# Two fused transformer blocks on one core: a reordered first block, a twelfth weight slot, and a second block that starts on rows that are not yet normalised

## The chip, the cores and the metric

The program runs on 1 core of one Trainium2 chip. The metric is the device time of one execution in microseconds (us). All arithmetic is 32-bit float. TensorE is called PE here, VectorE DVE, ScalarE ACT, GpSimd POOL and SyncE SP.

## The reference, cut to what matters

The input is x, 256 rows of 1024 features; 16 learned meta rows are put ahead of it for the first mixer.

```python
# block 1
h = concat(meta, x)                                   # 16 + 256 rows
p = rmsnorm(h, norm1_g) @ w_in                        # 1024 -> 6144: q f i og lx ly ga gb
o_a = hgrn2(q, f, i, og)                              # 4 heads of 128, gated linear recurrence
o_b = rglru(conv4(lx), ly)                            # two 128x128 products per block, then a scan
m = sigmoid(ga) * (o_a @ w_up_a) + sigmoid(gb) * (o_b @ w_up_b)
h = h + m @ w_out
h = h + moe(rmsnorm(h, norm2_g))                      # 32 experts, 2 per row, 6 MB of weights each
x = rmsnorm(h, final_g)[16:]
# block 2
p = rmsnorm(x, norm1_g_2) @ w_in_2                    # 1024 -> 7680: 3 q, 3 k, 3 v, uv, ga, gb
m = sigmoid(ga) * (attn(q, k, v) @ w_proj_attn) + sigmoid(gb) * (gmlp(uv) @ w_proj_sgu)
x = x + m @ w_out_2
x = x + (silu(n @ w_gate) * (n @ w_up)) @ w_down      # n = rmsnorm(x, norm2_g_2), 2816 wide
return rmsnorm(x, final_g_2)
```

Every expert is evaluated for the up to 32 rows routed to it, so all 201 MB of expert weights are read.

## The kernel before, in words

The order on each engine is written by hand, and every dependence is a named semaphore. SP issues nearly all weight loads, in units of 2 MB (`load`, L310). Block 1 has 18 units in a ring of 6 slots; the experts have 96 units, 12 for each group of four experts, in 11 slots (`NSLOT`, `MOE_SLOTS`), five of which lie in the work area and come free as block 1 ends; block 2 has 36 units in the ring again. A load into a slot waits for the semaphore of the work that read it last (`used1`, `used2`, `unit_used`). SP waits for `params_issued` before its first load, that is, until ACT has issued the loads of x, of the meta rows and of all small parameters.

Block 1 starts with a normalisation of the rows: ACT squares and sums each tile of rows (L1000), POOL turns the sum into the reciprocal root (L442, L444), DVE scales the rows (L1258), PE transposes them (L504), DVE copies them out of PSUM with the gain (L1278) into `hnT`. Then PE goes through the units: `project_rows` (L537) makes rows, 16 meta rows and two tiles of 128, `project_cols` (L528) makes feature-major columns in four chunks, each in one of PSUM banks 0 to 3 and each evacuated by ACT (`evac`, L1015). A matmul of 32-bit floats is two PE instructions. Between the units stand the recurrence's own products: the end keys and values (L552, L557, with DVE copies L1351, L1354, L1360 between them), the levels (L577), the heads' outputs, their sums of squares (L605), and the 16 LRU products (L617), each followed by a sigmoid of ACT (L1081). The columns `gb` are projected after the LRU products. `up_a` (L628) goes to banks 0 to 3 and waits for the last evacuation; `up_b` (L636) goes to banks 4 to 7. DVE merges the two (`merge`, L1468 to L1470), and `out_projection` (L651) waits for all eight merged columns:

```python
            pe.wait_ge(S("evac"), n_out[0])
            pe.wait_ge(S("oa_ready"), 1)
...
                        if t == 0 and k == 0:
                            pe.wait_ge(S(ready), total)
```

Routing follows, and then the experts, four at a time: gate, up, gather for the next four, down, and a weighted sum into banks 4 to 7 (`combine`, L727). The last group's down weights come in column halves (L755).

After the last `combine` DVE copies the result to `h` (L1672), the final norm of block 1 is applied to the rows (L1677), then the first norm of block 2 is taken with squares, root, scaled rows, transposes and gain, into `hn2`, and ACT makes a copy `hn2c` with columns sorted by residue class (L1171). Only then does block 2's first unit start (L537). The evacuated q and k rows are rotated by DVE and transposed (L844); attention, the gated unit, merge, output projection and feed-forward (L961, L1801, L651) follow.

## Time and profile before

| | us |
|---|---|
| median of 3 runs | 1340.3 (1337.79 to 1340.61) |
| the profiled execution, own time | 1339.59 |
| its span | 1337.8 |
| PE busy | 1117.2 (84%) |
| DVE busy | 253.9 (19%) |
| ACT busy | 179.3 (13%) |
| POOL busy | 18.3 (1%) |
| chain that ended last: PE | 69% of the span |
| chain that ended last: DMA | 23% of the span |

Busy time is summed over the span; the chain follows the work back from the last instruction, so it says which engine or transfer set the end at each moment. The chain lies on PE up to 350.5 us, on the expert loads up to 769.1 us, and on PE again to the end, with short pieces of DVE, ACT and POOL between them.

### The profile page before, as it was taken

The numbers are of one execution on the slowest core, as the hardware profiler recorded it, in microseconds if no ns is written. First come the engines' busy times: TensorE is split into PE (matmuls) and PEld (weight loads), VectorE is DVE, ScalarE is ACT, GpSimd is POOL, SyncE is SP. The second block draws the span as 40 slices with busy tenths as digits, with TensorE's granted clock in tenths as the row PEclk, the third lists the DMA queues.
The fourth block names the chain that finished last, engine by engine and source line by source line (L and its number), as shares of the span: only waits on it lengthen the run. The fifth ranks groups of instructions, "written<-read, shape, count | busy, mean of one in ns | idle before, by whom it ended". The sixth has DMA issues, their size and how long they took to land.

```text
span 1337.8 us, 12093 instructions
## 1 busy us (share of the span) xinstructions
PE 1117.2 (84%) x5319; PEld 696.7 (52%) x5319; DVE 253.9 (19%) x585; ACT 179.3 (13%) x354; POOL 18.3 (1%) x47
## 2 busy tenths in 40 slices
PE   6989999898965666465575679999999889999997
PEld 2778988765422212121231234444688648888643
DVE  4233243423110000000000041101353310000000
ACT  2213325101100000000000031111333010000000
POOL 1000000000000000000000010000000000000000
PEclk9989999997977867787787889999999989999999
DMA  8732334484799999999999995336223334453200
GB/s 299 243 126 91 110 108 163 185 319 184 309 428 427 429 425 427 430 426 428 428 429 427 394 348 182 126 126 219 90 101 126 126 108 146 139 178 137 95 16 16
DMA packets 89631, 318.31 MB, mean 238 GB/s; under 512 B 8684, under 2 KB 34392, under 8 KB 78824
## 3 DMA queue, kind: packets, MB, share of 16 engines
q1 hardware_dynamic: 81536, 313.53, 59.9%
q10 hardware_dynamic: 8040, 3.96, 1.1%
q8 instruction: 44, 0.72, 0.2%
q14 instruction: 11, 0.09, 0.0%
HBM read 316.43 MB, written 1.05 MB: 237 GB/s over the span
## 4 chain that ended last, share of the span: by engine, by line
PE 69%; DMA 23%; DVE 3%; ACT 2%; SPq 1%; issue 1%; ACTq 0%; POOL 0%; POOLq 0%; DVEq 0%
PE bank L537 13%; PE bank L961 12%; PE bank L528 11%; PE bank L651 10%; PE bank L708 5%; DMA ring<-in_w_gate 5%; DMA ring<-in_w_up 5%; DMA ring<-in_w_down 4%; PE bank L859 4%; DMA arena<-in_w_gate 4%; DMA arena<-in_w_down 3%; DMA arena<-in_w_up 2%; PE bank L941 2%; PE bank L636 2%; PE bank L746 2%; SPq L310 1%
## 5 line engine op out<-in xcount | busy, mean ns | idle before, releaser
L708 PE MATMUL bank<-ring,arena 128*32 128x512 f32 x512 | 128.0, 733 | 61.3 <-DMA ring<-in_w_up 27.7
L537 PE MATMUL bank<-ring,arena 128*128 128x512 f32 (+1 forms) x400 | 175.4, 598 | 1.6 <-DVE arena L1278 1.6
L708 PE MATMUL bank<-arena 128*32 128x512 f32 x384 | 128.0, 738 | 55.7 <-DMA ring<-in_w_gate 21.2
L528 PE MATMUL bank<-arena,ring 128*128 128x256 f32 (+1 forms) x704 | 157.8, 386 | 1.2 <-DVE arena L1360 1.2
L961 PE MATMUL bank<-arena,ring 128*128 128x256 f32 x704 | 154.7, 383 | 0.8 <-DVE arena L1278 0.8
L528 PEld LDWEIGHTS bank<-arena,ring 128*128 128x128 f32 x704 | 134.6, 192 | 23.0 <-DVE arena L1360 1.5
L961 PEld LDWEIGHTS bank<-arena,ring 128*128 128x128 f32 x704 | 135.5, 193 | 20.0 <-DVE arena L1278 1.2
L651 PE MATMUL bank<-ring,arena 128*128 128x512 f32 x304 | 131.2, 593 | 6.5 <-DVE arena L1470 5.4
L537 PEld LDWEIGHTS bank<-ring,arena 128*128 128x128 f32 (+1 forms) x400 | 73.9, 187 | 97.1 <-issue 94.6
L651 PEld LDWEIGHTS bank<-ring,arena 128*128 128x128 f32 x304 | 57.5, 190 | 78.8 <-issue 78.8
L708 PEld LDWEIGHTS bank<-ring,arena 128*32 128x32 f32 x512 | 31.8, 132 | 113.3 <-issue 113.3
L708 PEld LDWEIGHTS bank<-arena 128*32 128x32 f32 x384 | 31.2, 132 | 96.0 <-issue 96.0
L746 PE MATMUL bank<-ring,arena 128*32 128x512 f32 x224 | 61.8, 700 | 19.2 <-DMA arena<-in_w_down 13.2
L746 PE MATMUL bank<-arena 128*32 128x512 f32 x224 | 61.8, 729 | 18.8 <-DMA ring<-in_w_down 12.7
L1015 ACT ACTIVATE arena<-bank 128x256 f32<-128x256 f32 (+3 forms) x85 | 37.8, 448 | 275.2 <-PE bank L537 149.9
L859 PE MATMUL bank<-arena,ring 128*128 128x256 f32 x256 | 59.4, 385 | 0.8 <-ACT arena L1015 0.8
L1589 DVE TENSOR_TENSOR h<-h,bank 128x512 f32<-128x512 f32 x8 | 5.5, 689 | 274.0 <-PE bank L708 260.6
L859 PEld LDWEIGHTS bank<-arena,ring 128*128 128x128 f32 x256 | 47.3, 190 | 10.3 <-issue 4.1
L1000 ACT ACTIVATE arena<-h 128x1024 f32<-128x1024 f32 x12 | 12.7, 1055 | 223.6 <-DVE h L1481 209.7
L1801 DVE TENSOR_TENSOR arena<-arena,bank 128x256 f32<-128x256 f32 x22 | 9.3, 422 | 146.4 <-ACT arena L1232 146.4
L746 PEld LDWEIGHTS bank<-ring,arena 128*32 128x32 f32 x224 | 15.0, 126 | 40.7 <-issue 40.0
L746 PEld LDWEIGHTS bank<-arena 128*32 128x32 f32 x224 | 15.3, 131 | 37.4 <-issue 37.4
(273 smaller groups left out, 871.2 us busy)
## 6 DMA issues: line engine op xcount, KB each, us to landing
ring<-in_w_in SPq DMA_DIRECT2D x27, 2048.0 KB, 9.2
ring<-in_w_up SPq DMA_DIRECT2D x20, 2048.0 KB, 35.0
ring<-in_w_gate SPq DMA_DIRECT2D x16, 2048.0 KB, 34.8
arena<-in_w_gate SPq DMA_DIRECT2D x16, 2048.0 KB, 33.9
ring<-in_w_down SPq DMA_DIRECT2D x14, 2048.0 KB, 32.6
arena<-in_w_down SPq DMA_DIRECT2D x14, 2048.0 KB, 35.5
arena<-in_w_up SPq DMA_DIRECT2D x12, 2048.0 KB, 32.8
ring<-in_w_ffn_gate SPq DMA_DIRECT2D x11, 1024.0 KB, 5.3
```

What stands on the lines that cost most here:

```text
L310: sp.dma_start(dst, src).then_inc(S(f"landed{s}"), 16)
L528: last = mm(b[:, 0:n], w3(s, KC)[:, k, m * P:(m + 1) * P], hn[:, k, lo:lo + n], start=(k == 0), stop=(k == KC - 1))
L537: last = mm(b[0:n, :], hn[:, k, lo:lo + n], w3(s, KC)[:, k, :], start=(k == 0), stop=(k == KC - 1))
L636: last = mm(bank[4 + m // 2][:, (m % 2) * T:(m % 2 + 1) * T], w3(up_b[k // 4], 4)[:, k % 4, m * P:(m + 1) * P], ly[:, k, :], start=(k == 0 ...
L651: last = mm(bank[2 * t + half][:, :], src[:, k, t * P:(t + 1) * P], w3(slots[k // 4], 4)[:, k % 4, half * 512:(half + 1) * 512], start=(k ...
L708: last = mm(bank[b][e * CAP:(e + 1) * CAP, :], xgT[:, k, e * CAP:(e + 1) * CAP], w[e][:, k, :], start=(k == 0), stop=(k == KC - 1))
L746: last = mm(bank[2 + half][e * CAP:(e + 1) * CAP, :], hT[:, k, e * CAP:(e + 1) * CAP], w[e][:, k, half * 512:(half + 1) * 512], start=(k = ...
L859: last = mm(b[:, 0:T], w3(gate_slot[0], KC)[:, k, (n % 4) * P:(n % 4 + 1) * P], hn2[:, k, :], start=(k == 0), stop=(k == KC - 1))
L941: last = mm(bank[lo + m // 2][:, (m % 2) * T:(m % 2 + 1) * T], w3(su, 4)[:, k, m * P:(m + 1) * P], src[:, k, :], start=(k == 0), stop=(k = ...
L961: last = mm(b[:, q * T:(q + 1) * T], w3(su, 2 * KC)[:, KC * q + k, (c % 2) * P:(c % 2 + 1) * P], hn2[:, k, :], start=(k == 0), stop=(k == ...
L1000: A_(junk[tile][0:n, :], src[0:n, tile, :] if tile < NT else meta[0:n, :], ACT.Square, accum_out=stat[0:n, col + tile:col + tile + 1]).the ...
L1015: A_(dst, src, func).then_inc(S("evac"), 1)
```

## The change

In block 1, x is loaded by SP ahead of the weights, and the first unit in two halves; the wait for the small parameters goes. PE transposes the raw rows, DVE puts the gain on them (`rT`), and the first unit is projected from these, with the row scale applied by ACT at the evacuation. The normalised `hnT` is made from `rT` by DVE with the scale spread over partitions by a product with ones. The meta rows' unit is projected in four column groups of PE, whose partial sums stay apart and are added by the key-value product with the keys repeated four times. The end-key transposes and products stand between chunks of the units `lx0` and `lx1`. Half of `gb0` is projected ahead of the LRU products. `up_a` goes to banks 4 to 7 and `up_b` to 0 to 3. ACT evacuates `gb1` before the LRU's square root. Both output projections start once six merged columns are there, and take the second tile's two halves one after the other.

A twelfth slot of 2 MB is its own tensor; room comes from a work area 80 words smaller and from `dynamic_dma_scratch_size=256` in place of the default.

At the end of the experts, the first 512 features of the result are copied, transposed raw and scaled by gain before the last expert unit is projected. Block 2's unit 0 starts on these; the other 512 features are transposed between its steps. The row scale (final norm times first norm of block 2) is applied by ACT at evacuation for units 0 to 6. DVE makes `hn2c` from `hn2` with the spread scale after unit 1, and PE waits for it (`classed`) before unit 2; `hn2` itself is scaled later, and PE waits for that before unit 9.

The diff, cut to its core (several semaphores are merged or renamed too, and the branch for more than 32 rows per expert is adapted; it isn't taken in the profiled execution):

```diff
-NSLOT = 11
-MOE_SLOTS = [0, 1, 6, 7, 8, 2, 3, 9, 4, 5, 10]
-B2_SLOTS = [4, 5, 0, 1, 2, 3]
-WORK = 4432
+NSLOT = 12
+MOE_SLOTS = [11, 0, 1, 6, 7, 8, 2, 3, 9, 4, 5, 10]
+B2_SLOTS = [0, 1, 2, 3, 4, 5]
...
+DMA_SCRATCH = 256
...
-            sp.wait_ge(S("params_issued"), 1)
+            for t in range(NT):
+                sp.dma_start(h[:, t, :], A["x"][0, t * P:(t + 1) * P, :]).then_inc(S(f"x_in{t + 1}"), 16)
...
                     sp.wait_ge(S(used1(u - RING)[0]), used1(u - RING)[1])
-                if name in W1_COL:
+                if u == 0:
+                    sp.dma_start(w3(s, KC)[:, 0:4, :], w1[:, 0:4, W1_COL[name]:W1_COL[name] + 512]) \
+                        .then_inc(S("half_landed"), 16)
...
-            turn_rows(((2, META), (0, P), (1, P)), "n1", xn, 3)
+            pe.wait_ge(S("gain_loaded"), 16)
+            tr(bank[7][:, 0:8], vecrows[0:8, :], ident[0:8, 0:8]).then_inc(S("vec_turned"), 1)
+            for t in range(NT):
+                pe.wait_ge(S(f"x_in{t + 1}"), 16)
+                for half in range(2):
+                    for c in range(4):
+                        k = 4 * half + c
+                        last = tr(bank[2 * t + half][:, c * P:(c + 1) * P], h[:, t, k * P:(k + 1) * P], ident[:, :])
+                    last.then_inc(S("x_turned"), 1)
+            pe.wait_ge(S("vec_loaded"), 16 * (len(VEC_ROWS) - 1))
+            tr(bank[6][:, 0:NVR], vecrows[0:NVR, :], ident[0:NVR, 0:NVR]).then_inc(S("vec_turned"), 1)
...
+            def project_meta(s):
+
+                b = out_bank()
+                for k in range(0, KC, 4):
+                    for c in range(4):
+                        last = mm(b[32 * c:32 * c + 32, :], hnT[:, k + c, 0:32], w3(s, KC)[:, k + c, :],
+                                  start=(k == 0), stop=(k == 4))
+                last.then_inc(S("projected"), 1)
+
+            pe.wait_ge(S("half_landed"), 16)
+            for t in range(NT):
+                b = out_bank()
+                pe.wait_ge(S("x_scaled"), 2 * (t + 1))
+                for k in range(KC):
+                    if t == 0 and k == 4:
+                        take1(0)
+                    last = mm(b[:, :], rT[:, k, t * P:(t + 1) * P], w3(0, KC)[:, k, :], start=(k == 0), stop=(k == KC - 1))
+                last.then_inc(S("projected"), 1)
+                if t == 0:
+                    turn_meta()
+                else:
+                    spread_rstd(0)
+                    spread_rstd(1)
+            pe.wait_ge(S("norm_done"), 2)
+            pe.wait_ge(S("hn_scaled"), NT)
+            project_meta(0)
             project_cols(take1(1), hnT, 0, TT)
             project_cols(take1(2), hnT, META, T)
-            project_cols(take1(3), hnT, 0, TT)
-
...
+            s3 = take1(3)
+            project_cols(s3, hnT, 0, TT, (0, 1))
+            turn_k(0)
+            project_cols(s3, hnT, 0, TT, (2, 3))
+            turn_k(1)
+            s4 = take1(4)
+            project_cols(s4, hnT, 0, TT, (0,))
+            kv(0)
+            kv(1)
+            project_cols(s4, hnT, 0, TT, (1, 2, 3))
...
-            project_cols(take1(4), hnT, 0, TT)
...
+            s11 = take1(11)
+            project_cols(s11, hnT, META, T, (0, 1))
             take1(10)
...
-            project_cols(take1(11), hnT, META, T)
+            project_cols(s11, hnT, META, T, (2, 3))
             project_cols(take1(12), hnT, META, T)
...
-            pe.wait_ge(S("evac"), n_out[0])
...
+            pe.wait_ge(S("lru_gates"), 16)
             pe.wait_ge(S("oa_ready"), 1)
...
-            last.then_inc(S("up_a"), 1)
-            pe.wait_ge(S("lru_gates"), 16)
+            last.then_inc(S("projected_a"), 1)
+            pe.wait_ge(S("evac"), n_out[0])
             pe.wait_ge(S("ob_ready"), 1)
             up_b = [take1(14), take1(15)]
             for m in range(KC):
+                if m >= 4:
+                    pe.wait_ge(S("merged"), m - 3)
                 for k in range(KC):
...
+                last.then_inc(S("projected_b"), 1)
...
-                for t in range(NT):
+                for k in range(total):
+                    if k % 4 == 0:
+                        slots.append(take(u0 + k // 4))
+                    pe.wait_ge(S(ready), max(k + 1, min(6, total)))
+                    for half in range(2):
+                        last = mm(bank[half][:, :], src[:, k, 0:P], w3(slots[k // 4], 4)[:, k % 4, half * 512:(half + 1) * 512],
+                                  start=(k == 0), stop=(k == total - 1))
+                last.then_inc(S("out_" + ready), 1)
+                for half in range(2):
                     for k in range(total):
-                        if t == 0 and k % 4 == 0:
-                            slots.append(take(u0 + k // 4))
-                        if t == 0 and k == 0:
-                            pe.wait_ge(S(ready), total)
-                        for half in range(2):
-                            last = mm(bank[2 * t + half][:, :], src[:, k, t * P:(t + 1) * P],
-                                      w3(slots[k // 4], 4)[:, k % 4, half * 512:(half + 1) * 512],
-                                      start=(k == 0), stop=(k == total - 1))
+                        last = mm(bank[2 + half][:, :], src[:, k, P:T],
+                                  w3(slots[k // 4], 4)[:, k % 4, half * 512:(half + 1) * 512],
+                                  start=(k == 0), stop=(k == total - 1))
                     last.then_inc(S("out_" + ready), 1)
...
-            combine((0,))
+            combine((0,)).then_inc(S("combined"), 1)
+
+            def turn_half(half, done="raw_turned"):
+
+                for t in range(NT):
+                    pe.wait_ge(S("y_added"), 1 if half == 0 else 2 + t)
+                    for c in range(4):
+                        last = tr(bank[half + t][:, c * P:(c + 1) * P], h[:, t, (4 * half + c) * P:(4 * half + c + 1) * P],
+                                  ident[:, :])
+                    last.then_inc(S(done), 1)
+
+            turn_half(0)
             down_columns(1, 2, take_moe(m + 11)).then_inc(S("unit_used"), 1)
             pe.wait_ge(S("y_copied"), 2 * QUADS - 1)
...
-            turn_rows(((0, P), (1, P)), "n3", [xn2[:, 0, :], xn2[:, 1, :]], 2)
-            pe.wait_ge(S("norm_done"), 2 * ROWS["n3"] + 4)
...
+            s0 = take2(0)
+            b0, b1 = out_bank(), out_bank()
+            pe.wait_ge(S("raw_done"), 2)
+            steps(s0, b0, 0, (0, 1))
+            turn_half(1)
+            steps(s0, b0, 0, (2, 3))
+            steps(s0, b1, 1, (0, 1, 2, 3))
+            pe.wait_ge(S("raw_done"), 3)
+            steps(s0, b0, 0, (4, 5, 6, 7)).then_inc(S("projected"), 1)
+            pe.wait_ge(S("raw_done"), 4)
+            steps(s0, b1, 1, (4, 5, 6, 7)).then_inc(S("projected"), 1)
...
             for n in range(11):
-                if n == 7:
+                if n == 2:
                     pe.wait_ge(S("classed"), 1)
-                project_rows(take2(n), tiles, hn2c if n in (7, 8) else hn2)
+                if n == 9:
+                    pe.wait_ge(S("classed"), 2)
+                if n:
+                    project_rows(take2(n), tiles, hn2c if n in (7, 8) else hn2)
+                if n == 1:
+                    pe.wait_ge(S("s_diag"), 2)
+                    for t in range(NT):
+                        last = mm(bank[7][:, t * P:(t + 1) * P], ones[:, :], s_diag[:, t, :], start=True, stop=True)
+                    last.then_inc(S("s_spread"), 1)
...
+            for t in range(NT):
+                dve.wait_ge(S("r_spread"), t + 1)
+                dve.wait_ge(S("x_scaled"), 2 * NT)
+                v.tensor_tensor(hnT[:, :, META + t * P:META + (t + 1) * P], rT[:, :, t * P:(t + 1) * P],
+                                bc(bank[(7, 3)[t]][:, 0:P], [P, KC, P], 1), ALU.mult).then_inc(S("hn_scaled"), 1)
...
-            act.wait_ge(S("lru_under"), 1)
-            A_(lrut, lrut, ACT.Sqrt).then_inc(S("lru_root"), 1)
             for c in range(4):
                 evac(gb[:, 4 + c, :], ACT.Sigmoid, n=T)
+            act.wait_ge(S("lru_under"), 1)
+            A_(lrut, lrut, ACT.Sqrt).then_inc(S("root"), 1)
...
+            def hold(half, t):
+
+                return v.tensor_copy(h[:, t, half * 512:(half + 1) * 512], bank[4 + 2 * t + half][:, :])
+
+            def scale_half(half, turned, done):
+                for t in range(NT):
+                    dve.wait_ge(S(turned[0]), turned[1] + t)
+                    v.tensor_tensor(hn2[:, 4 * half:4 * half + 4, t * P:(t + 1) * P],
+                                    bank[half + t][:, :].rearrange("p (c t) -> p c t", c=4),
+                                    bc(gains3[:, 4 * half:4 * half + 4], [P, 4, P], 2), ALU.mult).then_inc(S(done), 1)
+
             for q in range(QUADS):
...
+                if q + 1 == QUADS:
+                    dve.wait_ge(S("combined"), QUADS)
+                    hold(0, 0)
+                    hold(0, 1).then_inc(S("y_added"), 1)
+                    scale_half(0, ("raw_turned", 1), "raw_done")
...
+            dve.wait_ge(S("combined"), QUADS + 1)
+            for t in range(NT):
+                hold(1, t).then_inc(S("y_added"), 1)
+            scale_half(1, ("raw_turned", 3), "raw_done")
...
+                if n == 0:
+                    dve.wait_ge(S("s_spread"), 1)
+                    link(v.tensor_copy(sbc, bank[7][:, 0:T]))
+                    for k in range(KC):
+                        last = v.tensor_tensor(hn2c[:, k, :].rearrange("p (c j a) -> p c j a", c=4, j=4),
+                                               hn2[:, k, :].rearrange("p (a j c) -> p c j a", j=4, c=4),
+                                               sbc.rearrange("p (a j c) -> p c j a", j=4, c=4), ALU.mult)
+                    last.then_inc(S("classed"), 1)
+            dve.wait_ge(S("projected"), B1_OUTS + 14)
+            v.tensor_tensor(hn2, hn2, bc(sbc, [P, KC, T], 1), ALU.mult).then_inc(S("classed"), 1)
```

## Rows read from the trace of the kernel before

**Rows 1.** The page: busy tenths of the DMA engines in 40 slices of the span.

```profile
DMA  8732334484799999999999995336223334453200
```

**Rows 2.** Windows: us, busy PE, PEld, DVE, ACT, POOL; granted clock, DMA share, GB/s.

```profile
15.00:20.00 5.00, 4.21 (x13) 2.12 (x12) 3.67 (x12) 1.00 (x3) 0.16 (x1) 1.00 1.05 387
...
340.00:350.00 10.00, 9.15 (x87) 3.22 (x90) 1.45 (x3) 3.00 (x3) 0.00 (x0) 1.00 0.55 205
...
400.00:500.00 100.00, 59.81 (x420) 22.60 (x408) 6.25 (x12) 4.42 (x7) 0.00 (x0) 0.80 1.01 428
```

**Rows 3.** Timeline of the start: start us, us, queue or engine, line, instruction, idle before.

```profile
7.64 61.91 SPq L310 DMA_DIRECT2D ring<-in_w_in  x9
...
17.88 22.79 PE L537 MATMUL bank<-ring,arena 128*16 128x512 f32 x48 [0.79 <-DVE arena L1278]
```

**Rows 4.** DMA issues: tile, engine, count, KB each, median us to landing.

```profile
h<-in_x ACTq DMA_DIRECT2D x2, 512.0 KB, 4.0
```

**Rows 5.** The chain that ended last, around the keys: start us, us, what.

```profile
40.67 43.15 PE bank L528 x192
...
83.82 0.45 PE bank L552 x4
...
92.81 16.83 PE bank L528 x64
...
113.21 13.82 PE bank L528 x64
```

**Rows 6.** Timeline of the end of the first mixer, the stretch 196 to 287 us.

```profile
196.41 1.88 PE L605 MATMUL bank<-arena,ones 128*128 128x512 f32 x4
...
202.02 6.83 ACT L1081 ACTIVATE arena<-bank,vec 128x272 f32<-128x272 f32 x16
...
207.40 1.22 DVE L1442 TENSOR_TENSOR arena<-arena 128x1024 f32<-128x1024 f32 x1
...
208.17 27.79 PE L528 MATMUL bank<-arena,ring 128*128 128x256 f32 x128
...
222.59 1.28 ACT L1089 ACT_TABLE_LOAD   x1
...
230.64 2.43 DVE L1449 TENSOR_TENSOR arena<-arena 128x2176 f32<-128x2176 f32 x1 [20.31 <-ACT arena L1091]
...
235.63 2.02 ACT L1094 ACTIVATE arena<-arena 128x2176 f32<-128x2176 f32 x1 [3.72 <-DVE arena L1451]
...
240.22 15.66 PE L628 MATMUL bank<-arena,ring 128*128 128x256 f32 x64 [4.26 <-ACT arena L1015]
...
245.49 2.29 DVE L1461 TENSOR_TENSOR arena<-arena 128x2048 f32<-128x2048 f32 x1
...
286.22 13.97 PE L651 MATMUL bank<-ring,arena 128*128 128x512 f32 x32 [2.71 <-DVE arena L1470]
```

**Rows 7.** Timeline of SP's queue: the first load that reuses an expert slot.

```profile
343.62 0.33 SPq L310 DMA_DIRECT2D ring<-in_w_down  x1
```

**Rows 8.** The chain that ended last, from the last expert load to block 2.

```profile
769.08 1.97 PE bank L755 x16
...
773.84 1.30 DVE h L1672 x2
...
786.62 27.73 PE bank L537 x64
```

**Rows 9.** Timeline of PE: the combine of the first column half.

```profile
765.52 1.98 PE L727 MATMUL bank<-h,arena 128*128 128x512 f32 x4
```

**Rows 10.** Timeline of SP's queue: the last expert loads and the first of block 2.

```profile
752.02 5.16 SPq L310 DMA_DIRECT2D arena<-in_w_down  x2
758.24 129.55 SPq L310 DMA_DIRECT2D ring<-in_w_in  x13
```

**Rows 11.** Timeline of block 2's end: a merge step, the last projection.

```profile
1061.65 0.42 DVE L1468 TENSOR_TENSOR arena<-arena,bank 128x256 f32<-128x256 f32 x1 [0.99 <-PE bank L941]
...
1254.23 75.77 PE L651 MATMUL bank<-ring,arena 128*128 128x512 f32 x176 [1.02 <-DVE arena L1801]
```

More of the change, by code:

```diff
@@ L366, in _ @@
                 elif s == 9:
[L367 removed]
+                    sp.wait_ge(S("projected_b"), KC)
                 elif s == 10:
@@ L1050, in _ @@
             level_exp(1)
-            for c in range(4):
-                evac(lx[:, 4 + c, 3:3 + TT], ACT.Copy, n=TT)
+            for c in range(5, KC):
+                evac(lx[:, c, 3:3 + TT], ACT.Copy, n=TT)
             level_exp(2)
@@ L1074, in _ @@
             act.wait_ge(S("o_mean"), 1)
-            A_(rsn, rsn, ACT.Sqrt).then_inc(S("o_root"), 1)
+            A_(rsn, rsn, ACT.Sqrt).then_inc(S("root"), 1)
+            for c in range(2):
+                evac(gb[:, c, :], ACT.Sigmoid, n=T)
             for b in range(KC):
@@ L1365, in seg @@
+            dve.wait_ge(S("end_decay"), 3)
+            dve.wait_ge(S("state"), 1)
+            for hd in range(HEADS):
+                last = v.scalar_tensor_tensor(out=St[:, 1, hd, :], in0=St[:, 0, hd, :],
+                                              scalar=egA[:, hd:hd + 1], in1=bank[7][:, hd * P:(hd + 1) * P],
+                                              op0=ALU.mult, op1=ALU.add)
+            last.then_inc(S("state"), 1)
             def seg(ap, m):
```

284 lines of the change are left out of this document (165 added, 119 removed).

## The prediction, on record before the changed kernel ran

> **What bounds the kernel now.** I read the page first: the DMA engines are nearly full from slice 12 to slice 24 and less than half busy in most others [rows 1]. The windows say how full: between 400 and 500 us they move 428 GB/s and PE is busy for 59.8 of 100 us [rows 2]. So the span has three stages: block 1, bound by PE and by waits between engines; the expert loads, bound by transfers; block 2, bound by PE. Then I read the chain of waits in order of time, to see in each stage which wait ends last. A saving in block 1 counts only if it also lets the expert stream start earlier. It does: the stream's first reuse of a slot is issued at 343.62 us [rows 7], right after the first expert product, and the window 340 to 350 is at 205 GB/s, not full [rows 2]. From there to the last landing at 769.08 [rows 8] the stream never pauses. Block 1 sets when it starts, its bytes set how long it lasts, and the path from the last landing to block 2's first product comes in full.
>
> All sums are against the profiled execution, 1339.6 us with a span of 1337.8; the median of the three runs is 1340.3.
>
> **Price of a unit.** 64 PE instructions of 512 columns take 27.73 us [rows 8], so one tile of 128 rows (16 instructions) is 6.93 and a unit of two tiles 13.87. A unit of 256 columns is 13.82 [rows 5]. The chain's 43.15 us for f, q and lx0 [rows 5] less 13.82 leaves 14.66 for each unit of 272 columns.
>
> **The start.** Before, the weights are issued at 7.64 and the first product starts at 17.88; 48 instructions end at 40.67 [rows 3, 5]. Two tiles are 13.87 of these 22.79 us. The other 8.9 are the meta rows, which cost as many instructions as a full tile (6.93), and 2.0 at the lower pace of the first few. After: x is issued on SP at about 1 us and lands 4 us later [rows 4]. The half unit behind it (1 MB at the 387 GB/s of these weights [rows 2]) needs 2.7 us more. I add 1.5 for the small parameters that now move at the same time, and take 9.5 for the first product. The bounds: 8 with no such cost, and 11.5 if the present lag of 10.2 us from issue to product stays. The raw transposes and the gain on DVE lie beside that transfer. Then 13.9 + 2.0 for two tiles. DVE multiplies 2 x 1024 columns by the spread scale (1.22 each [rows 6]) with PE waiting, 2.6 with its semaphores. The meta unit is 16 instructions in four column groups, a shape that the last expert unit runs in 1.97 [rows 8]. End: 9.5 + 13.9 + 2.0 + 2.6 + 1.9 = 29.9, against 40.67. Gain 10.8 (8.8 to 12.5). ACT's squares and POOL's roots are done long before these two tiles end; their cover gone, each tile's root would cost about 1 us.
>
> **The end keys.** From 83.82 to the end of the next unit at 109.64 the chain takes 25.8 us, where the unit alone is 14.66: 9.0 of transposes and products with DVE copies between them, and 2.2 because the unit after them, on 16.83, begins at the low clock [rows 5]. After, DVE's copies lie beside half units of 7 us. What stays is PE's own work: two times four transposes and two times eight product instructions, by 0.45 for four [rows 5] some 2.7. Gain 8.4 (6 if the clock falls all the same). DVE now reaches the first level differences 7 us later in the unit, but the first level stands 9 us behind that and needs only four DVE steps and two exponentials.
>
> **The LRU stage.** Before: sums of squares end at 198.3, sixteen products run at ACT's pace (6.83 us for its 16 sigmoids) until gb starts at 208.17, its two units end at 235.96, PE idles 4.26 and `up_a` takes 15.66 instead of 13.8, to end at 255.9 [rows 6]. After: half of gb0 (6.9) from 198.1 hides the DVE mean and the square root; the products end about 211.4, the rest of gb at 232.2, and `up_a`, which no longer waits for the evacuation, at 246.0. Late next is `ob_ready`. ACT's exponentials start behind gb0's last evacuation at 218.8, take 8.05 as now (222.59 to 230.64), DVE 5.0, so `lru_under` is at 231.9; but ACT first evacuates the last gb chunk (232.6), loads the table (1.28) and takes the root (2.02): 235.9. From the root's end at 237.65 to `ob_ready` at 247.78 are 10.1 us now [rows 6]; after: 246.0. This meets `up_a`'s end with nothing to spare. Gain 9.9 (7.5 to 10.1).
>
> A switch of table costs 1.28 us by the trace [rows 6]. The Trainium skill (ScalarE: Activation LUTs, What ACT_TABLE_LOAD costs) puts 2.66 us on every switch, a drain included. By that `ob_ready` would come 1.4 us later and the gain would be 8.5; the sum goes by the trace.
>
> **First merge and output.** PE waits 2.71 us for the last two merges before `out_projection` [rows 6]; it now needs six of eight, which are there. At the end only one of two additions from PSUM is left; two copies of that shape take 1.30 [rows 8], and I take the same. Gain 2.7 + 0.6 = 3.3.
>
> Block 1 in all: 10.8 + 8.4 + 9.9 + 3.3 = 32.4.
>
> **The twelfth slot.** Slot 11 needs no wait, so it fills in block 1, where the DMA engines have room. At the first reuse twelve units have landed and not eleven: one unit of 2.097 MB at 428 GB/s [rows 2], 4.9 us. It is worth nothing if the stream turns out not to be full.
>
> **The seam.** L is the last landing (769.08). Now block 2's unit 1 starts at 786.62 + 13.87 = 800.5, which is L + 31.4. After: the first combine ends at 767.5 (L - 1.6) [rows 9], two copies 1.3 [rows 8], eight transposes 0.9: PE is free at L + 0.7, so the last unit starts 0.7 late and ends at L + 2.5. DVE copy 0.7, combine 2.0: L + 5.3. PE's own read of the overflow flag was hidden; 1 us for it (0 to 1.5): SP's queue reads the same flag between its last expert load (752.02 + 5.16) and block 2's first at 758.24, 1.06 us [rows 10]. The unit's 16 + 16 instructions 13.9, eight transposes 0.9, semaphores 0.2: L + 21.3. The unit's weights stand directly behind the last expert unit in SP's queue, 5.4 us at 387 GB/s: L + 5.4, in time. Norms, roots and `row_scale` run beside the unit. Gain 10.1; bounds 5, if PE starts it at the low clock and the flag costs more, and 10.6.
>
> **The new wait.** PE reaches unit 2 some 1.2 us after unit 1 (spread, eight transposes). DVE copies the spread scale and makes eight class-sorted products; 0.42 each is the nearest row [rows 11], 3.8 with the copy, from 0.5 us after unit 1. Price 3.1 us; 2.3 if they overlap, 6 if the sorted read is slower and the clock falls. Behind the wait are all later units of PE, and nobody else.
>
> **Block 2's end.** The same wait of 2.7 us before its `out_projection` goes, as do half the additions twice (0.6 each), and 1.0 before the last projection [rows 11]. Gain 4.9.
>
> **Sum.** 32.4 + 4.9 + 10.1 - 3.1 + 4.9 = 49.2. 1339.6 - 49.2 = 1290.4; I say 1291.
>
> **Rivals.**
> A. Block 1 gives back nearly a quarter of its gain, because the waits removed turn into others on DVE or ACT (start bound by the weights as now, `ob_ready` late, the clock low after the key products). By the low bounds: 8.8 + 6 + 7.5 + 3 = 25.3, so 1298. The tie at `ob_ready` speaks for it; against it, every engine but PE is under a third busy.
> B. The seam doesn't pay: PE runs unit 0 at the low clock in pieces and the `classed` wait costs 6: 5 + 3 us lost, 1299. With A, 1306.
> C. The raw start does nothing, since block 2's weights arrive too late. They come behind 2 MB of transfers at 387 GB/s; if unit 0 landed at L + 17, the present start, the gain of 10.1 would be gone: 1301. Speaks against it: the queue is in order and now block 2 waits for DVE and not for a load.
> D. Slower than before: the expert stream itself loses rate, because the slots, their addresses and the descriptor room change. 84 units follow the first reuse. It decides from 49.2 / 84 = 0.59 us per unit, 382 GB/s and below. At 350 GB/s a unit is 6.0 us: 1291 + 92 = 1383. The stream ran at 428 GB/s in eleven slots of two tensors alike, which speaks against.
> E. More than the sum: the start at 8, the tight waits all met: 1281 to 1284.
>
> **How the numbers follow.** Forecast (1285 to 1296) 0.55, A 0.14, B 0.10, C 0.06, A and B together 0.04, E 0.08, D 0.03. The bounds of the terms together are some 8 us on either side. The range runs from 1282 to 1304 and leaves out half of E, A with B, and D. Within 0.2% (2.7 us) is about what a measurement of this kernel can't tell from no change; to end there, A, B and C together wouldn't do. Faster 0.97, same 0.01, slower 0.02.
>
> **What would show it.** The first L537-type product near 9.5 us and unit f starting near 30; no gap of over 1 us at the keys; `up_b` starting near 226.6 (255.7 - 10.8 - 8.4 - 9.9); the first reuse of an expert slot near 311; full windows until about 732 (769.1 - 32.4 - 4.9); block 2's first product 6 to 7 us behind the last landing and unit 1 at 21; one new PE wait of 3 us on DVE before unit 2. Wrong would be: windows below 428 GB/s in the stream, DVE or ACT behind a new PE wait of over 2 us in block 1, or a granted clock of 0.5 in unit 0 of block 2.

## The result, and the profile after

The changed kernel takes 1307.8 us (median of 4 runs, 1306.26 to 1308.26), the kernel before 1340.2 in the same session: a ratio of 0.976, 95% interval 0.9743 to 0.9777. That is faster, as forecast, but 16.8 us above the 1291 and 3.8 above the range. The profiled execution took 1307.79 with a span of 1305.8; against 1339.59 it saves 31.8 where the sum said 49.2. So 17.4 us are to be found.

The expert stream is as it was, by the windows of the changed kernel (us, busy PE, PEld, DVE, ACT, POOL, granted clock, DMA share, GB/s), against 428 in [rows 2]:

```profile
400.00:500.00 100.00, 61.06 (x416) 24.02 (x420) 5.22 (x10) 4.88 (x7) 0.00 (x0) 0.81 1.01 427
```

The chain that ended last, first 100 us (start us, us, what):

```profile
5.67 5.15 DMA arena<-in_final_g
...
11.18 8.58 PE bank L600 x16
...
35.65 5.52 ACTq L1149
...
41.20 4.35 ACTq L1149
...
45.58 2.00 ACTq L1149
...
47.61 1.28 ACT L1153
...
49.73 22.85 PE bank L555 x96
72.58 0.44 PE bank L616 x4
73.02 7.34 PE bank L555 x32
80.35 0.44 PE bank L616 x4
80.79 3.67 PE bank L555 x16
84.46 1.78 PE bank L622 x16
86.25 11.00 PE bank L555 x48
97.25 3.57 PE bank L651 x32
```

The reader is to see three things. The keys behave as predicted: from 72.58 to 97.25 the chain has only PE, 24.67 us, 22.0 of unit chunks and 2.7 of key work. The first product starts at 11.18 by the chain (11.02 on the timeline), not 17.88 [rows 3]. And between the two stands a piece that the prediction doesn't have: ACT's queue (ACTq), issuing the loads of the router's weights until 47.6.

The timeline of the changed kernel at the end of the first mixer and at the first expert product, which answers to [rows 6, 7]:

```profile
184.02 1.88 PE L678 MATMUL bank<-arena,ones 128*128 128x512 f32 x4
...
192.64 7.50 PE L692 MATMUL bank<-arena,ring 128*128 128x272 f32 x32
...
220.69 13.98 PE L707 MATMUL bank<-arena,ring 128*128 128x256 f32 x64
234.63 27.86 PE L717 MATMUL bank<-arena,ring 128*128 128x256 f32 x128
...
316.90 1.92 PE L782 MATMUL bank<-extra,arena 128*32 128x512 f32 x16 [0.85 <-DVE arena L1740]
```

No product waits here any more. The first reuse of an expert slot is issued at 318.88 us, 24.7 earlier than in [rows 7], where 32.4 were forecast.

The seam and the start of block 2, timeline of PE (an "issue" in brackets: idle, and no releaser in the trace):

```profile
740.20 1.92 PE L838 MATMUL bank<-arena 128*32 128x512 f32 x16
742.94 1.98 PE L810 MATMUL bank<-h,arena 128*128 128x512 f32 x4 [0.81 <-DVE h L1811]
750.33 3.75 PE L934 MATMUL bank<-ring,arena 128*128 128x512 f32 x4 [5.41 <-issue]
...
755.58 12.31 PE L934 MATMUL bank<-ring,arena 128*128 128x512 f32 x28
767.74 13.90 PE L564 MATMUL bank<-ring,arena 128*128 128x512 f32 x32
...
786.75 15.59 PE L564 MATMUL bank<-ring,arena 128*128 128x512 f32 x32 [3.80 <-DVE arena L1909]
...
803.05 3.17 PE L564 MATMUL bank<-ring,arena 128*128 128x512 f32 x7
```

The last expert product starts 28.9 us earlier than in [rows 8]: 24.7 from block 1 and some 4.9 from the slot, less 0.7 for the transposes ahead of it. Then PE does nothing for 5.41 us, and the first four instructions of unit 0 take 0.94 us each, the 28 later ones 0.44. The windows show the granted clock at 0.50 behind the pause, its lower level of 1.2 GHz:

```profile
750.00:755.00 5.00, 4.67 (x10) 2.53 (x11) 0.03 (x1) 0.00 (x0) 0.00 (x0) 0.50 1.05 386
...
760.00:770.00 10.00, 10.00 (x25) 4.49 (x24) 6.91 (x30) 1.59 (x4) 1.61 (x6) 1.00 0.96 349
```

The new wait of 3.80 us stands behind unit 1 and its transposes, ahead of the product at 786.75.

### The profile page after: what moved, and what is told of

It is laid out like the page before. It is cut to its first block, busy times and chain, and to the rows that moved or that the text cites. A ratio compares the mean times of both kernels' runs of the same rounds, so it can differ in the third digit from the quotient of the medians.

```text
span 1305.8 us, 12127 instructions
## 1 busy us (share of the span) xinstructions
PE 1106.2 (85%) x5328; PEld 694.6 (53%) x5328; DVE 262.3 (20%) x599; ACT 176.6 (14%) x346; POOL 16.2 (1%) x50
## 4 chain that ended last, share of the span: by engine, by line
PE 69%; DMA 24%; SPq 2%; DVE 2%; ACTq 1%; ACT 1%; issue 1%; POOL 0%; POOLq 0%; DVEq 0%
DMA arena<-in_w_gate 22%; PE bank L1084 12%; PE bank L555 11%; PE bank L564 11%; PE bank L734 5%; PE bank L729 5%; PE bank L791 5%; PE bank L973 4%; PE bank L1065 2%; PE bank L717 2%; SPq L319 2%; PE bank L934 1%; PE bank L600 1%; DMA ring<-in_w_down 1%; PE bank L651 1%; PE bank L782 1%
## 5 line engine op out<-in xcount | busy, mean ns | idle before, releaser
L791 PE MATMUL bank<-arena 128*32 128x512 f32 x336 | 124.7, 721 | 51.2 <-DMA ring<-in_w_up 51.2
L564 PE MATMUL bank<-ring,arena 128*128 128x512 f32 x320 | 140.4, 598 | 3.8 <-DVE arena L1909 3.8
L791 PE MATMUL bank<-ring,arena 128*32 128x512 f32 x448 | 124.7, 720 | 0.0
L791 PE MATMUL bank<-extra,arena 128*32 128x512 f32 x112 | 61.9, 717 | 63.9 <-DMA arena<-in_w_gate 63.9
L564 PEld LDWEIGHTS bank<-ring,arena 128*128 128x128 f32 x320 | 60.9, 192 | 78.3 <-issue 74.1
L829 PE MATMUL bank<-arena 128*32 128x512 f32 x224 | 61.6, 712 | 38.1 <-DMA arena<-in_w_down 37.6
L791 PEld LDWEIGHTS bank<-extra,arena 128*32 128x32 f32 x112 | 13.9, 130 | 108.5 <-issue 108.4
L729 PE MATMUL bank<-ring,arena 128*128 128x512 f32 x152 | 65.7, 592 | 0.0
L734 PE MATMUL bank<-ring,arena 128*128 128x512 f32 x152 | 65.7, 592 | 0.0
L829 PE MATMUL bank<-ring,arena 128*32 128x512 f32 x224 | 61.6, 712 | 0.0
L973 PEld LDWEIGHTS bank<-arena,ring 128*128 128x128 f32 x256 | 47.3, 190 | 10.2 <-issue 3.9
L1135 ACT ACTIVATE arena<-bank 128x256 f32<-128x256 f32 (+2 forms) x69 | 28.4, 414 | 176.8 <-PE bank L555 96.8
L734 PEld LDWEIGHTS bank<-ring,arena 128*128 128x128 f32 x152 | 28.9, 190 | 36.4 <-issue 36.4
L729 PEld LDWEIGHTS bank<-ring,arena 128*128 128x128 f32 x152 | 28.9, 190 | 35.1 <-issue 34.2
```

What stands on the lines that cost most here:

```text
L564: last = mm(b[0:n, :], hn[:, k, lo:lo + n], w3(s, KC)[:, k, :], start=(k == 0), stop=(k == KC - 1))
L729: last = mm(bank[half][:, :], src[:, k, 0:P], w3(slots[k // 4], 4)[:, k % 4, half * 512:(half + 1) * 512], start=(k == 0), stop=(k == tota ...
L734: last = mm(bank[2 + half][:, :], src[:, k, P:T], w3(slots[k // 4], 4)[:, k % 4, half * 512:(half + 1) * 512], start=(k == 0), stop=(k == ...
L791: last = mm(bank[b][e * CAP:(e + 1) * CAP, :], xgT[:, k, e * CAP:(e + 1) * CAP], w[e][:, k, :], start=(k == 0), stop=(k == KC - 1))
L829: last = mm(bank[2 + half][e * CAP:(e + 1) * CAP, :], hT[:, k, e * CAP:(e + 1) * CAP], w[e][:, k, half * 512:(half + 1) * 512], start=(k = ...
L973: last = mm(b[:, 0:T], w3(gate_slot[0], KC)[:, k, (n % 4) * P:(n % 4 + 1) * P], hn2[:, k, :], start=(k == 0), stop=(k == KC - 1))
```

## The experiments

Twelve kernels, in three groups of four, each group on one chip beside the kernel before. The changed kernel's own row is repeated from above.

| edit | median us | ratio to before, 95% interval |
|---|---|---|
| the change | 1307.8 | 0.976 (0.9743 to 0.9777) |
| router's loads on SP | 1302.1 | 0.9718 (0.9700 to 0.9736) |
| no branch on PE | 1299.2 | 0.9687 (0.9667 to 0.9707) |
| wait ahead of unit 7 | 1300.2 | 0.9696 (0.9669 to 0.9722) |
| eleven slots | 1312.3 | 0.979 (0.9773 to 0.9808) |
| flag read early | 1305.5 | 0.9742 (0.9726 to 0.9759) |
| short skipped path | 1299.1 | 0.9703 (0.9678 to 0.9727) |
| prefetch hint | 1300.5 | 0.9705 (0.9689 to 0.9721) |
| loads on SP, parameters later | 1300.6 | 0.9706 (0.9687 to 0.9724) |
| three edits | 1290.0 | 0.9628 (0.9615 to 0.9641) |
| router's loads late on ACT | 1302.3 | 0.9722 (0.9707 to 0.9736) |
| gb0 undone | 1309.6 | 0.9781 (0.9766 to 0.9796) |
| three edits, loads late | 1290.3 | 0.963 (0.9617 to 0.9643) |

### ACT's queue: where block 1 lost

In SP's queue, ahead of the seventh unit, and out of ACT's:

```diff
+                if u == RING:
+                    sp.dma_start(rw[:, :, 0:4], A["w_group"][0].rearrange("(p k) e -> p k e", k=KC)).then_inc(S("rw_loaded"), 16)
...
-            act.dma_start(rw[:, :, 0:4], A["w_group"][0].rearrange("(p k) e -> p k e", k=KC)).then_inc(S("rw_loaded"), 16)
...
```

> The five loads of the router's weights go from ACT's queue to SP's, behind the sixth unit. Theory (ACT's queue is the stall): the changed kernel leaves PE idle for 2.76 us at 49.73 because ACT issues these five loads from 34.8 to 47.6 us before it can evacuate the first f chunk. Without them ACT evacuates at about 35, the 2.76 us go and PE keeps its high clock behind them: the end keys, the first merge and the end all come 4 to 5 us earlier, 1303. Rival (the loads aren't it, the table load and the parameter exponentials are late, or DVE is): the stall shrinks by under 1 us, 1307. Second rival: SP is held by the five issues so long that the seventh unit of weights lands late and PE waits for it in block 1: 1308 or more.

In the timeline of this run's PE there is no stall, and the first expert product comes 6.96 us earlier than in the changed kernel's (316.90):

```profile
29.54 36.08 PE L560 MATMUL bank<-arena,ring 128*128 128x272 f32 x160
...
309.94 1.93 PE L787 MATMUL bank<-extra,arena 128*32 128x512 f32 x16 [0.85 <-DVE arena L1741]
```

So it is ACT's queue, and it took more than the stall of 2.76 us in the trace. The run shows why: unit f starts at 29.54 here and at 32.04 in the changed kernel, whose clock was at 0.50 from 12 to 15 us. These 2.50 us, the stall of 2.76 and 1.70 at the low clock behind the stall are the 6.96. In the run with the wait moved and in the one with eleven slots the first unit also ended some 2.3 us earlier, and their stall was 5.24 and 5.47 us instead of 2.76. The same holds for all eight kernels that keep these loads in this place: unit f starts between 29.5 and 32.2 us, but the issues end between 47.3 and 48.0 and PE goes on between 49.5 and 50.2. ACT's queue sets when PE goes on, whatever the start gains, and so the low clock at the start cost the changed kernel nothing by itself. The timeline of ACT and its queue in the kernel before had the same block, covered:

```profile
41.38 10.13 ACTq L1027 DMA_DIRECT2D route<-in_w_router  x4
...
53.13 0.39 ACT L1015 ACTIVATE arena<-bank 128x272 f32<-128x272 f32 x1
```

PE began f at 40.51 and had four banks, so it first needed one back at 40.51 + 14.66 = 55.2; ACT freed it at 53.5, 1.6 us to spare. After the change PE needs it at 32.0 + 14.7 = 46.7, and ACT, whose last three issues take 12.0 us, frees it at 49.6.

> The five loads of the router's weights stay on ACT's queue but stand ahead of its wait for the first merge, at about 225 us, where ACT has nothing to do for 39 us. Theory R1 (the issues are long because the DMA engines are full of 2 MB units): each takes 0.4 to 0.7 us there, as the first two of the changed kernel did, not 12 us for the last three. Theory R2 (a load of many small pieces takes its issuer 2.5 us and more by itself): 10 us or more for the five, still hidden. The time by both: the 7 us of block 1 as in the run with the loads on SP, 1301 to 1302; 1 us less if the seventh unit of weights, which SP issued later in that run, had mattered.

The time was as forecast. The issues, which began at 216.3 us and not at 225, were neither: 0.64 us for the first, 6.22 and 1.85 for the two pairs behind it, 8.7 in all, at a mean DMA share of 0.84. It was 10.8 us at 0.97 in the kernel before, 13.4 at 1.02 in the changed kernel, and 18.7 at 0.96 on SP in the first run. On ACT fuller engines go with longer issues, but the run on SP doesn't fit that, and what an issue waits for stays open.

### The start: the half unit holds the first product

The edit adds to the first run: the last parameter transpose and its wait stand behind the first tile.

```diff
-            pe.wait_ge(S("vec_loaded"), 16 * (len(VEC_ROWS) - 1))
-            tr(bank[6][:, 0:NVR], vecrows[0:NVR, :], ident[0:NVR, 0:NVR]).then_inc(S("vec_turned"), 1)
...
                 if t == 0:
+                    pe.wait_ge(S("vec_loaded"), 16 * (len(VEC_ROWS) - 1))
+                    tr(bank[6][:, 0:NVR], vecrows[0:NVR, :], ident[0:NVR, 0:NVR]).then_inc(S("vec_turned"), 1)
                     turn_meta()
```

> On top of the router's loads on SP (1302.1 us), the transpose of the small parameters and its wait move behind the products of the first tile. Theory S1 (the last parameter row holds PE: idle 1.0 to 2.0 us, and a low clock after it): the first product starts at 9.6 us, when the half unit lands, instead of 10.5 to 11; 1 us earlier, up to 2.5 where the low clock went with it: 1300 to 1301. Theory S2 (the weights hold it: the half unit lands 7.9 us behind its issue at 1.71, and the second half at 12.9): PE starts earlier and then waits 1 to 1.5 us inside the first tile for the second half, and the time stays at 1302.

Timeline of PE, first the run with the loads on SP alone, then this one:

```profile
10.22 7.04 PE L605 MATMUL bank<-ring,arena 128*128 128x512 f32 x16
```

```profile
9.44 8.14 PE L603 MATMUL bank<-ring,arena 128*128 128x512 f32 x16 [0.24 <-DMA ring<-in_w_in]
```

PE starts 0.8 us earlier, as soon as the half unit is there, and needs 1.1 us more for the tile. The wait for the second half that S2 expected isn't in the trace. PE's weight loads (PEld) show where the 1.1 us lie, here the third instruction of the tile and the ninth, which is the first to read the second half:

```profile
10.46 0.34 PEld L603 LDWEIGHTS bank<-ring,arena 128*128 128x128 f32 x1 [0.52 <-issue]
...
13.55 0.19 PEld L603 LDWEIGHTS bank<-ring,arena 128*128 128x128 f32 x1 [0.24 <-issue]
```

Up to 11.8 us the loads come as slowly as in the changed kernel at a granted clock of 0.50, 0.85 us apart; from there they come every 0.43 us, with no gap at the ninth. The granted clock reads 1.00 all along, so the cause of the slow instructions stays open, and neither S1's gain nor S2's wait is shown. The median is 1.5 us lower, but the block is not shorter by the trace (this run's clock fell at 28 to 31 us instead), so nothing is credited to the edit.

### The seam: not the flag, but the branch

```diff
-            over = pe.value_load(idx[0:1, 40:41], min_val=0, max_val=T)
-            with pe.If(over > CAP):
-                pe.wait_ge(S("raw_done"), 2)
...
-                pe.wait_ge(S("over_held"), 2)
```

> PE's read of the overflow flag and its branch are left out, and with them PE's part of the overflow passes, which these inputs never enter; the other engines keep theirs. Theory A (the branch costs it: flag read, compare and fetching the instructions behind the skipped part): the 5.41 us in which PE does nothing ahead of block 2's first product shrink to under 1 us, and with the pause the low clock behind it goes as well: 5 to 7 us earlier, 1301 to 1303. Theory B (PE waits for the weights of block 2's first unit, which come behind the saturated transfers): the gap stays over 4 us and the time at 1307 to 1308.

PE's timeline of this run:

```profile
742.55 1.98 PE L810 MATMUL bank<-h,arena 128*128 128x512 f32 x4 [0.81 <-DVE h L1782]
744.43 1.98 PE L905 MATMUL bank<-ring,arena 128*128 128x512 f32 x4
...
759.14 13.90 PE L564 MATMUL bank<-ring,arena 128*128 128x512 f32 x32
```

There is no pause and no low clock. From the last expert unit's first product to unit 1 it is 19.3 us (739.81 to 759.14) against 27.5 (740.20 to 767.74): 8.2 us. The pause is 5.4 of them; unit 0 itself takes 14.71 us from its first product to unit 1 (744.43 to 759.14) and took 17.41 in the changed kernel (750.33 to 767.74), so the low clock behind the pause is the other 2.7. Theory B is out: unit 0's weights were there at 744.4, and PE took them without a pause (the DMA view has them 15.9 us behind their issue at 728.85, at 744.8 in the changed kernel). Three more runs divide the pause. In the expectation of the second, "16 stay" should read 8: the edit leaves 8 of 64 gate and up products and 8 of 32 down products.

```diff
+            over = pe.value_load(idx[0:1, 40:41], min_val=0, max_val=T)
             turn_half(0)
...
-            over = pe.value_load(idx[0:1, 40:41], min_val=0, max_val=T)
```

> Leaving out both the read of the overflow flag and the branch took PE's 5.41 us pause away; this tells the two apart. PE reads the flag into its register ahead of the transposes of the first half, where it waits 1.4 us for DVE anyway; the branch stays where it was. Theory A1 (the read is the cost, as the prediction priced it, only higher): the pause ahead of block 2's first product shrinks to 1 or 2 us and most of 8 us comes back, 1300 to 1302. Theory A2 (the branch itself and the instructions behind it are the cost): the pause stays at 4.4 us or more, the time at 1306 to 1308.

```diff
-                    for j in range(4):
-                        products(0, j, j)
-                    for j in range(4):
-                        last = products(1, j, 4 + j)
-                    last.then_inc(S("over_gate_up"), 1)
+                    products(0, 0, 0).then_inc(S("over_gate_up"), 1)
...
-                    for j in range(4):
-                        last = down(j, j)
-                    last.then_inc(S("over_down"), 1)
+                    down(0, 0).then_inc(S("over_down"), 1)
```

> The flag is read and branched on as in the changed kernel, but PE's skipped overflow path is made short: of its 64 gate and up products 16 stay, of its 32 down products 8; these inputs never enter the path. Theory A2 in the form that PE must fetch the instructions at a target far behind the skipped part when the branch is taken: with the target nearer it is there already, the pause falls from 5.41 to 1 or 2 us, 1300 to 1302. Rival (a taken branch costs PE the same however far it goes, or the flag read does): the pause stays at 5 us, 1306 to 1308.

```diff
+            ahead = pe.mark_branch_hint_location()
             combine((0,)).then_inc(S("combined"), 1)
...
-            with pe.If(over > CAP):
+            pe.br_cmp(over, CAP, "no_over", "is_over", "IS_LE").branch_hint(ahead)
```

> Everything is computed as in the changed kernel. PE gets a prefetch hint for the branch, put ahead of the first combine, some 7 us before the branch. Theory A2 (fetch of the instructions behind the skipped part): the pause falls to what the read and the compare take, 0.5 to 1.5 us, and unit 0 runs at the high clock: 1300 to 1301. Rival (the read of the flag is the cost, or the hint doesn't reach over the distance): the pause stays at 5 us, 1307.

The first product of block 2 in the timelines of the three, in this order:

```profile
750.54 3.62 PE L934 MATMUL bank<-ring,arena 128*128 128x512 f32 x4 [4.53 <-issue]
```

```profile
743.47 1.98 PE L810 MATMUL bank<-h,arena 128*128 128x512 f32 x4 [0.81 <-DVE h L1805]
745.34 1.98 PE L928 MATMUL bank<-ring,arena 128*128 128x512 f32 x4
```

```profile
744.75 1.98 PE L938 MATMUL bank<-ring,arena 128*128 128x512 f32 x4
...
750.30 10.46 PE L938 MATMUL bank<-ring,arena 128*128 128x512 f32 x24 [0.98 <-issue]
```

The read of the flag costs 5.41 - 4.53 = 0.9 us, what the prediction had (1.0). The other 4.5 are the branch, and only where its target lies far off: with fewer instructions to skip, or with a hint 7 us ahead, they are gone, and the read of the flag is hidden as well. The DMA queues of the changed kernel between 747 and 749 us, inside the pause (queue, kind: packets, MB, share of 16 engines), hold two packets of instructions:

```profile
q8 instruction: 1, 0.02, 3.3%
q14 instruction: 1, 0.01, 1.1%
```

They alone prove nothing: the run with the short path has none from 743 to 747.5 us, but one in each of these two queues from there to 749, while PE multiplies without a pause, and the view doesn't say which engine they are for. That the pause is a fetch is argued from the two edits that remove it. The Trainium skill (Runtime: NRT & Kernel Launch, Instruction fetch mechanics) says that prefetch is sequential, and that a taken branch whose target isn't in the current window of pages waits for a fetch. These runs agree with that rule; the page gives no time for it, and here it is 4.5 us beside saturated DMA engines. The hint has a price: 0.98 us of new pause, at the same product in all three kernels that carry it; the reason is open.

### The wait for the sorted features

```diff
-                if n == 2:
+                if n == 7:
                     pe.wait_ge(S("classed"), 1)
```

> PE's wait for the class-sorted features moves from ahead of block 2's unit 2 to ahead of unit 7, the first that reads them. Theory (the wait costs what the trace shows: 3.80 us idle and 1.9 us for the next unit at the low clock): unit 2 follows unit 1 and its transposes at once, 5 to 6 us earlier, 1302. Rival (DVE is now the next bound: its eight sorted products of 4.1 us delay the rotation of unit 1, so PE waits for the transposes of q and k behind unit 2): 2 to 3 us come back there and the time is 1304 to 1305.

PE's timeline of this run from unit 1 to unit 3:

```profile
768.42 13.90 PE L564 MATMUL bank<-ring,arena 128*128 128x512 f32 x32
...
783.48 13.90 PE L564 MATMUL bank<-ring,arena 128*128 128x512 f32 x32
...
798.08 13.90 PE L564 MATMUL bank<-ring,arena 128*128 128x512 f32 x32
```

From unit 1 to unit 3 it is 29.66 us (768.42 to 798.08) against 35.31 (767.74 to 803.05) in the changed kernel: 5.65 us, of which 3.80 is the wait and 1.7 the low clock behind it (15.59 for unit 2 against 13.90). The rotation that was to come late makes nobody wait. The median gives 7.5, but its four runs lie between 1297.8 and 1303.1, so the trace's number is the one to keep. It may be a low one: in the ten traced kernels that have this wait the low clock behind it cost unit 2 1.7 or 1.8 us three times, here among them, and 2.6 to 3.2 seven times.

### The slot, and the half unit of gb

```diff
-NSLOT = 12
-MOE_SLOTS = [11, 0, 1, 6, 7, 8, 2, 3, 9, 4, 5, 10]
-B2_SLOTS = [0, 1, 2, 3, 4, 5]
+NSLOT = 11
+MOE_SLOTS = [0, 1, 6, 7, 8, 2, 3, 9, 4, 5, 10]
+B2_SLOTS = [4, 5, 0, 1, 2, 3]
```

> The twelfth slot alone is undone: eleven slots in the order of the kernel before, everything else as changed. Theory (the stream is full from the first reuse, one unit more ahead of it is worth 2.097 MB at 428 GB/s, 4.9 us): the last expert product 4.9 us later than 740.3, 1312.7. Rival (the slot gives nothing because the DMA engines have no room for it in block 1, or the order of slots holds the stream anyway): 1308. If it is more than 5.5 us the slot had also filled pauses in the stream.

The last expert product moves by 5.62 us, from 740.20 to 745.82; 0.69 of this comes from block 1, where the first expert product stands at 317.59 against 316.90. The other 4.9 are the slot, what the sum said; the median moves by 4.5.

```diff
-            s11 = take1(11)
-            project_cols(s11, hnT, META, T, (0, 1))
             take1(10)
...
-            project_cols(s11, hnT, META, T, (2, 3))
+            project_cols(take1(11), hnT, META, T)
```

ACT's two evacuations go with them.

> One part of the change undone: all of gb0's products and evacuations stand behind the recurrence's sixteen gate products again, as in the kernel before; the banks, the other waits and the order of the rest stay changed. Theory (the half unit hid the mean on DVE, the root and two table loads on ACT): from the end of the sums to the first product of gb it took 9.9 us before; 9.9 + 6.9 for the half unit is 16.8, against 14.2 now: the LRU stage and the end 2.6 us later, 1310.4. Rival L1 (what the second projection waits for comes late as well, as the kernel before showed with 4.3 us): 4 to 6 us later, 1312 to 1314. Rival L2 (the half unit hid nothing, the stage is bound by the recurrence's chain of DVE and ACT): 1308.

PE's timeline of this run, from the sums to the second projection, and behind it the second projection in the kernel before:

```profile
182.49 1.88 PE L678 MATMUL bank<-arena,ones 128*128 128x512 f32 x4
185.79 2.07 PE L690 MATMUL bank<-arena,ring 128*128 128x272 f32 x8 [1.43 <-issue]
188.63 5.77 PE L690 MATMUL bank<-arena,ring 128*128 128x272 f32 x24 [0.77 <-ACT arena L1201]
...
235.79 27.86 PE L715 MATMUL bank<-arena,ring 128*128 128x256 f32 x128
```

```profile
255.72 27.79 PE L636 MATMUL bank<-arena,ring 128*128 128x256 f32 x128
```

From the sums to the second projection it is 53.3 us against 50.6 (184.02 to 234.63): 2.7, as the theory says; the median is 1.8 higher. Before, it was 59.3 (196.41 to 255.72), so the stage gains 8.7. The reordering of gb is 2.7 of it, and the rest is the first projection, which no longer waits 4.26 us and takes 13.98 instead of 15.66.

### All together

> All of the computation, with three of the edits together: the router's loads on SP behind the sixth unit, the wait for the sorted features ahead of unit 7, and the prefetch hint for PE's branch. Theory (three separate losses at three places, so they add): 5.7, 7.5 and 7.3 us below 1307.8, 1287; by the traces of the three alone 6.6 + 5.6 + 7.1 below a span of 1305.8, 1286.5, which is 1288.5 with what lies around it. Rival (part of each was the low clock, which then falls somewhere else): 1292 to 1295.

> All of the computation, as the run with three edits, but with the router's loads late on ACT's queue instead of SP's. Theory (the place of the loads doesn't matter once they are out of the first 50 us): within 1.5 us of the run with three edits, 1287 to 1288.5. Rival (SP's 19 us for the five issues held the seventh unit, or the small loads slow the full queue): 1 to 2 us faster than that run.

Both compute all that the reference asks. They take 1290.0 and 1290.3 us, 0.9628 (0.9615 to 0.9641) and 0.963 (0.9617 to 0.9643) of the kernel before, so they beat both kernels. The losses are three, at three places. By the medians they add but for 2.7 us, by the traces fully: a span of 1286.5 us was expected and 1286.9 came. The place of the router's loads doesn't matter once they are off ACT's queue in the first 50 us; on SP they are still issued there, from 24.6 to 42.9 us. The timeline of the first of the two at the seam, with the hint's 1.00:

```profile
738.73 1.96 PE L943 MATMUL bank<-ring,arena 128*128 128x512 f32 x4
...
744.28 10.46 PE L943 MATMUL bank<-ring,arena 128*128 128x512 f32 x24 [1.00 <-issue]
754.58 13.90 PE L569 MATMUL bank<-ring,arena 128*128 128x512 f32 x32
```

## Why the prediction was right and wrong

**Where 17.4 us went.** ACT's queue 7.0 (316.90 to 309.94). The seam 6.9: the prediction's stretch from the last unit's product at L + 0.7 to unit 1 at L + 21.3 is 20.6, the trace has 27.5. The wait `classed` 2.6 (5.65, not 3.1). The LRU stage 1.2. Together 17.7; of the terms that came out better than forecast the largest is block 2's end, 5.4 from unit 3 to the end of the span where 4.9 was forecast.

**The start.** The first product was forecast for 9.5 and came at 11.0; with the parameters out of the way it is 9.44, so the 1.5 us for the parameter loads and the half unit were right in size, and the transposed parameters, which PE's queue has ahead of the first tile, were missed. Unit f was forecast for 29.9: it came at 29.54 where the first product started at 10.22 and the clock stayed high, and at 32.04 in the changed kernel. The step that failed is the one behind it. "Gain 10.8 (8.8 to 12.5)" was booked as if all that stood behind the first unit moved with it. ACT's issues don't: they begin behind the first unit but end at 47.3 to 48.0 us whenever that is. The issues stood in the trace of before, with 1.6 us to spare. This is the prediction's rival A by size (25.3 against 24.7 measured) and in its general form, a removed wait that turns into one on ACT, but by none of the three waits that it named; that the sizes meet is luck.

**The end keys and the first merge.** Right. The stretch is 24.67; without the old waits it gains 8.4, as forecast. The first output projection follows the merge without a wait, and so does the second.

**The LRU stage.** 9.9 forecast, 8.7 measured. The tie at `ob_ready` held: DVE's last step before it ends at 234.53, and PE goes from `up_a` to `up_b` at 234.63 without a wait. The sixteen products, at ACT's pace, take 7.3 us and not the 6.4 of the sum. The prediction's other number, 8.5 by the table switch of 2.66 us that the Trainium skill (ScalarE: Activation LUTs, What ACT_TABLE_LOAD costs) states, lies nearer to the 8.7, but not for its reason: each switch took 1.28 us in this trace too, and PE never waited for the root.

**The twelfth slot.** Right, shown by undoing it. The stream kept 427 GB/s, so rival D is out. So is rival C: the weights were there at 744.8, 5.4 us behind the last landing, just where the sum had them.

**The seam.** The mechanism is right and its gain is real: without the branch unit 1 starts 19.3 us behind the last unit's first product, 1.3 better than forecast. The step that failed is "PE's own read of the overflow flag ... 1 us for it". The read is 0.9. What was left out is the branch behind it, since the price was taken from SP's 1.06 us [rows 10], and SP skips a dozen lines where PE skips 130 matmuls. In the kernel before, the same branch lay under the 8.36 us in which PE waited for the scaled rows of block 2. Then the low clock took 2.7 us more in unit 0.

**The new wait.** The mechanism was right; the size was off: eight sorted products took 4.13 us, 0.52 each, where 0.42 was the nearest row, and the clock fell behind the wait, the far bound of 6 that the prediction kept. It need not be paid at all at this place.

**The range.** Seam and `classed` wait lost together what rival B had, and a little more (9.5 us, not 8), and block 1 lost what rival A had. A and B together, 1306, held 0.04 and lay outside. They were taken as separate accidents, but block 1 and the seam have one pattern: a wait removed from PE uncovers what lay under it, here a queue's issues and a branch.

## What to carry to other kernels

When a wait is removed, list what every engine's queue did during it, DMA issues and branches among them, for each has its own end and won't move with PE. A gain at the start counts only as far as the next engine that stays in place: compare when each bank is needed back with when it is freed. A branch over a long skipped path on a busy engine is a cost of its own; put it under a wait, make the path short, or announce the jump.

## What the runs showed of the hardware that was not expected

- A taken branch on PE over the long overflow path cost 4.5 us, with 130 matmuls skipped (116 products of two PE instructions each and 14 transposes); over some 50 it cost nothing that shows, and neither with a prefetch hint 7 us ahead, which adds a pause of 1.0 us further on.
- Five loads of 16 and 32 KB, in pieces of 16 and 32 bytes, held the issuing queue for 8.7 to 18.7 us; the first of the five took 0.6 us on ACT, early and late alike, and 7.8 on SP. In eight kernels that begin them on ACT between 31.7 and 34.4 us, the last issue ends between 47.3 and 48.0.
- PE's granted clock fell to 0.50 for some 3 to 7 us after idle stretches of 2.0 us (the start), 5.4 us (the seam) and 3.8 us (the wait); such a fall cost 1.7 us at the start, 2.7 at the seam, and 1.7 to 3.2 behind the same wait of 3.8 us in ten kernels. An idle stretch of 2.31 us, ahead of the meta rows' products in all kernels but the one before, was followed by a fall in three of thirteen.
